# Longer fillings on TensorE at sixteen places, and sparse attention with its minima and exponentials one pair ahead and its value products two behind

## The chip, the cores and the metric

The kernel runs on one core of a Trainium2 chip. The time is the device time of one execution in microseconds (us). TensorE does the matrix products, VectorE (DVE in the rows), ScalarE (ACT) and GpSimd (POOL) the rest, SyncE starts the transfers. The trace gives, for every stretch, the clock that TensorE was granted, as a share of 2.4 GHz: it is either 1.00 (2.4 GHz) or 0.50 (1.2 GHz), and a mean between the two says how the stretch divides.

## The reference

The program is a small network on 512 tokens of width 1024, batch 1: two layers of a first block (attention, a gated delta net, convolution, a feed-forward net, with an RMS norm ahead of and behind each half), one layer with a recurrent time mix and a feed-forward net, and one with sparse attention, a short convolution and a mixture of experts. Cut to the parts that the change touches:

```
def rms_norm(x, w):   y = x * rsqrt(mean(x*x) + eps);  return y * w

# first block, for l in range(2)
h = rms_norm(x, pre_mix);   u = h @ w_in;  ...  y = mixers(u) @ w_out
x = x + rms_norm(y, post_mix)
h = rms_norm(x, pre_mlp);   y = square(relu(h @ w_ff1)) @ w_ff2
x = x + rms_norm(y, post_mlp)

# sparse attention of the last layer: 8 query heads, 2 key heads of 64, 512 tokens
for each head:
    o_cmp = softmax(masked(q @ k_cmp.T)) @ v_cmp      # 31 compressed keys
    o_slc = softmax(masked(q @ k_slc.T)) @ v_slc      # causal, up to 512 keys
    o_win = softmax(masked(q @ k_win.T)) @ v_win      # causal, up to 512 keys
    y = g0 * o_cmp + g1 * o_slc + g2 * o_win
```

## The kernel before

All is float32; the large products are made of three products of rounded halves (`high`, `low`; L501 to L503), tile by tile of 128 x 512. The network is a row of **phases**. A phase (L165) is a block in which each engine has its own list of instructions, tied by semaphores; at its end all engines meet twice (L169, L172), and no engine starts the next phase before the slowest has arrived.

**Fillings.** `fill_in` (L235) issues n products of a constant 128 x 128 tile into a bank that nobody reads. They compute nothing. They stand where TensorE has no work and waits for others. They are in TensorE's list, so the phase can't end before they are done. The change alters these counts:

- `rms_norm` (L242): TensorE adds up the squares (L286), then fills (L289) while ScalarE takes the root (L278) and VectorE makes the reciprocal (L300) and eight products (L306). With `add_to` (behind each feed-forward net of the first block: twice) VectorE makes eight more sums (L311), and the filling is twice as long. Without `add_to` it is called seven times: ahead of the two first-block layers, ahead of both halves of the last two layers, and at the very end.
- `add_norm` (L315, twice): the norm behind the mixers, the addition, and the next norm in one phase; its second filling is L362.
- `linear` (L409) with a `source`: at its start ScalarE and VectorE split the first weights (L518, L561) and the source (L554, L597), and TensorE fills (L507). If the first weights were already split in the phase before (`primed == SPLIT`) only the source is left to do. The two calls with `LOADED` are the output projections of the last two layers (L2230, L2798).
- `compress` (L2289): the filling L2399, while VectorE makes the short convolution (L2281, L2285).

**Sparse attention** (L2420) goes over 4 **tiles** j of two heads each, in each over 4 query blocks t, and for each over 2 branches: 32 **pairs** q, each a pair of heads. Eight pairs make a tile; t grows from 0 to 3 within it, two pairs each, and the work of a pair is (t + 1) x 128 keys wide. For each pair:

- `scored` (TensorE, L2583 and L2586): the scores, into two of four score banks. It runs two pairs ahead and waits until `exponent` of the pair that had the banks is done.
- `top` (VectorE, L2711): the minimum of each row. `exponent` (ScalarE, L2490): the exponentials.
- `transposed` (TensorE, L2597): turns them, into two banks. `take_turned` copies the first bank on ScalarE (L2499), the second on VectorE (L2720), into `turned`.
- `apply` (TensorE, L2615; for every other pair L2610 too, the compressed branch): the products with the values, into a product bank of a **group** (the two branches of one query block). There are two product banks; the next group but one waits for `rows_done` of the older.
- per group: `weigh` (VectorE, L2727 to L2732), `first_part` (ScalarE, L2517), `other_parts` (VectorE, L2740, L2745; gives `rows_done`), `turn_rows` (TensorE, L2624), `take_rows` (ScalarE, L2523).
- per tile, for the next one: `rotate` and `scale_query` at the tile's first pair, `score_c` and `top_of_c` at its third, `exponent_c` and `mask_c` at its fourth, `turn_c` and `take_turned_c` at its fifth and seventh (L2510).

The order on each engine is written out by hand in a loop over q. TensorE in step q (L2637): `scored(q + 2)`, the tile's or group's extra work, `apply(q - 1)`, a filling of one product (L2666), `transposed(q)`.

## Time and profile before

| | us |
|---|---|
| runs (three) | 4427.88, 4421.81, 4433.57; median 4427.88 |
| the profiled execution, its own time | 4435.43 |
| its span, first to last instruction | 4433.5 |
| TensorE busy | 4132.3 (93%) |
| VectorE, ScalarE busy | 1579.9, 1300.1 |
| mean granted clock over the span | 0.933 |
| sparse attention, first to last matrix product | 3293.57 to 3487.27 |

The span is nearly the whole time; what lies around it is 1.9 us. "Busy" on TensorE includes the fillings. A matrix product takes twice as long at clock 0.50, so a stretch can be busy and slow at once: the busy share must be read together with the granted clock. In the rows, `x30` is the number of instructions merged into one row, the bracket at the end is the idle time of the engine ahead of it and what ended it, and `PEq L172` is the meeting of all engines at a phase's end. A matrix product in plain float32 is counted as two instructions, one in rounded halves (L239, L501) as one.

### The profile page before, as it was taken

How to read it: one execution, taken by the hardware profiler on the slowest of the kernel's cores; microseconds unless marked ns; L12 is line 12 of the kernel's file. 1: busy time of each engine (PE TensorE's matmuls, PEld its weight loads, DVE VectorE, ACT ScalarE, POOL GpSimd, SP SyncE). 2: the span in 40 equal slices, each digit the busy share in tenths (PEclk: the TensorE clock that was granted, in tenths of full speed). 3: DMA queues.
4: the chain of work that ended last, by engine and by line, in shares of the span. 5: the costliest groups of instructions: out<-in, count | busy, mean ns of one | idle time of the engine just before them, and what ended most of it. 6: DMA issues, size and time to landing. Idle time of an engine off the chain costs nothing. (4 is left out here: it accounts for less than half of the span.)

```text
span 4433.5 us, 57036 instructions
## 1 busy us (share of the span) xinstructions
PE 4132.3 (93%) x22339; PEld 3461.1 (78%) x22339; DVE 1579.9 (36%) x2702; ACT 1300.1 (29%) x2253; POOL 206.9 (5%) x169
## 2 busy tenths in 40 slices
PE   8999999999999999999997899999988889999999
PEld 5787876777678887677765777787756689999998
DVE  2365535233236553523326543332233421111212
ACT  2364533231246453323123322221213311111111
POOL 0151100000024100000000000000000000000000
PEclk9998989999999898999998899999987889999999
DMA  3100012221200001222120012232220034454443
GB/s 121 43 1 1 0 38 76 93 86 49 93 33 1 1 0 38 86 85 95 57 85 15 1 39 76 81 105 68 96 76 1 21 127 161 176 193 164 156 168 125
DMA packets 51478, 324.88 MB, mean 73 GB/s; under 512 B 6528, under 2 KB 7424, under 8 KB 20352
## 3 DMA queue, kind: packets, MB, share of 16 engines
q1 hardware_dynamic: 51328, 322.85, 20.7%
q8 instruction: 98, 1.61, 0.1%
q14 instruction: 52, 0.43, 0.0%
HBM read 319.68 MB, written 2.10 MB: 73 GB/s over the span
## 5 line engine op out<-in xcount | busy, mean ns | idle before, releaser
L501 PE MATMUL bank<-high 128*128 128x512 f32 x2480 | 976.5, 394 | 43.9 <-DVEq L591 22.8
L502 PE MATMUL bank<-low,high 128*128 128x512 f32 x2480 | 973.8, 393 | 0.0
L503 PE MATMUL bank<-high,low 128*128 128x512 f32 x2480 | 972.6, 392 | 0.0
L501 PEld LDWEIGHTS bank<-high 128*128 128x128 f32 x2480 | 471.4, 190 | 149.8 <-DVEq L591 25.6
L503 PEld LDWEIGHTS bank<-high,low 128*128 128x128 f32 x2480 | 470.9, 190 | 99.4
L502 PEld LDWEIGHTS bank<-low,high 128*128 128x128 f32 x2480 | 471.3, 190 | 97.8
L561 DVE TENSOR_TENSOR low<-weight_ring,high 128x2048 fp32r<-128x2048 f32 (+1 forms) x144 | 319.3, 2218 | 545.8 <-ACT high L518 545.8
L3110 PE MATMUL bank<-chosen,glu_ring 128*128 128x176 f32 x2816 | 422.0, 313 | 0.0
L3110 PEld LDWEIGHTS bank<-chosen,glu_ring 128*128 128x128 f32 x2816 | 420.1, 190 | 0.0
L518 ACT ACTIVATE high<-weight_ring 128x2048 fp32r<-128x2048 f32 (+1 forms) x144 | 266.7, 1854 | 266.8 <-PE bank L503 233.0
L239 PE MATMUL bank<-filler 128*128 128x512 f32 x819 | 247.6, 446 | 23.9 <-PEq L172 23.2
L239 PEld LDWEIGHTS bank<-filler 128*128 128x128 f32 x819 | 167.7, 209 | 77.5 <-issue 41.3
L3121 PE MATMUL bank<-hidden,down_ring 128*128 128x176 f32 x1408 | 211.3, 313 | 0.0
L3121 PEld LDWEIGHTS bank<-hidden,down_ring 128*128 128x128 f32 x1408 | 210.4, 190 | 0.0
L1414 DVE TENSOR_TENSOR joint<-bank,level_masks 128x512 f32<-128x512 f32 x224 | 153.9, 691 | 146.7 <-PE bank L1433 146.7
L741 POOL TENSOR_TENSOR y<-y,scaled 128x512 f32<-128x512 f32 x120 | 149.8, 1277 | 1007.7 <-ACT scaled L775 1007.7
L3199 DVE TENSOR_TENSOR hidden<-silu,bank 128x176 f32<-128x176 f32 x88 | 29.8, 338 | 390.6 <-ACT silu L3167 390.6
L569 DVE TENSOR_TENSOR gated<-gated,bank 128x512 f32<-128x512 f32 x86 | 59.0, 686 | 285.0 <-ACT gated L525 159.0
L3167 ACT ACTIVATE silu<-bank 128x176 f32<-128x176 f32 x88 | 27.9, 318 | 445.8 <-PE bank L3110 445.8
L1446 PE MATMUL bank<-weight_ring,joint 128*128 128x128 f32 x1152 | 151.8, 276 | 0.0
L622 ACT ACTIVATE u<-bank 128x512 f32 (+1 forms) x84 | 50.3, 599 | 330.4 <-PE bank L503 330.4
L1446 PEld LDWEIGHTS bank<-weight_ring,joint 128*128 128x128 f32 x1152 | 139.5, 192 | 0.9
(497 smaller groups left out, 4904.6 us busy)
## 6 DMA issues: line engine op xcount, KB each, us to landing
glu_ring<-in_w_expert SPq DMA_DIRECT2D x88, 1024.0 KB, 4.9
weight_ring<-in_w_ff SPq DMA_DIRECT2D x64, 1024.0 KB, 5.0
down_ring<-in_w_expert_down SPq DMA_DIRECT2D x64, 704.0 KB, 5.0
weight_ring<-in_w_in SPq DMA_DIRECT2D x22, 1024.0 KB, 4.8
weight_ring<-in_w_ffe SPq DMA_DIRECT2D x22, 1024.0 KB, 4.9
weight_ring<-in_w_downe SPq DMA_DIRECT2D x16, 704.0 KB, 4.1
weight_ring<-in_w_ino SPq DMA_DIRECT2D x11, 1024.0 KB, 4.8
weight_ring<-in_w_ine SPq DMA_DIRECT2D x9, 1024.0 KB, 5.0
```

Of the source, the lines that this page charges most:

```text
L239: nc.tensor.matmul(bank[:, :], tile, tile.unsqueeze(1).broadcast_to([P, SEQ // P, P]), start=True, stop=True)
L501: nc.tensor.matmul(mem.bank[b][:, :], whole, high[:, k, :], start=(k == 0), stop=False)
L502: nc.tensor.matmul(mem.bank[b][:, :], whole, low[:, k, :], start=False, stop=False)
L503: last = nc.tensor.matmul(mem.bank[b][:, :], rest, high[:, k, :], start=False, stop=(k == kt - 1))
L518: nc.scalar.activation(w_high[:, s, :], mem.ring[:, s, 0:size], ACT.Copy).then_inc(high_ready[s], 1)
L561: nc.vector.tensor_tensor(w_low[:, s, :], mem.ring[:, s, 0:size], w_high[:, s, :], ALU.subtract).then_inc(low_ready[s], 1)
L569: nc.vector.tensor_tensor(whole, whole, mem.bank[b][:, :], ALU.mult).then_inc(taken[b], 1)
L741: nc.gpsimd.tensor_tensor(y[:, c, :], y[:, c, :], scaled[:, n % CONV_SLOTS, :], ALU.add).then_inc(added, 1)
L1414: nc.vector.tensor_tensor(chunks(joint[:, n, :]), chunks(turn_bank(i)[:, :]), mask, ALU.mult) \
L1446: last = nc.tensor.matmul(product_bank(i)[:, c], joint[:, n, c], matrix[:, n, c], start=True, stop=True)
L3110: last = nc.tensor.matmul(two(low[s])[:, half, :], glu_ring[:, s, at:at + P], chosen[:, k, :], start=(k == 0), stop=(k == KD - 1))
L3121: last = nc.tensor.matmul(two(high[m // 2])[:, m % 2, :], down_ring[:, s, k * P:(k + 1) * P], hidden[:, k, :], start=(k == 0), stop=(k == ...
```

## The change

Three things. Fillings: 30 products become 42 and 60 become 84 in the norms, 5 become 12 in `linear` where the first weights are loaded only, 30 become 52 in `compress`, and sparse attention gets two new fillings at its start (4 behind `rotate(0)`, 8 behind `score_c(0)`). Second, the order of VectorE and ScalarE in sparse attention: `top` and `exponent` are called one pair further ahead, and `take_turned` of a pair in its own step. Third, TensorE applies pair q - 2 instead of q - 1 in step q, with `turned` six wide instead of four, and waits for `high_taken` ahead of the filling, a wait that `apply(q - 1)` held before.

```diff
@@ rms_norm
-            fill_in(nc, mem, mem.bank[1], 30 if add_to is None else 60)
+            fill_in(nc, mem, mem.bank[1], 42 if add_to is None else 84)
@@ add_norm
-            fill_in(nc, mem, mem.bank[2], 30)
+            fill_in(nc, mem, mem.bank[2], 42)
@@ linear
-                fill_in(nc, mem, mem.bank[n_banks - 1], 5)
+                fill_in(nc, mem, mem.bank[n_banks - 1], 5 if primed == SPLIT else 12)
@@ compress
-            fill_in(nc, mem, turn_banks[0], 30)
+            fill_in(nc, mem, turn_banks[0], 52)
@@ sparse_attention, ScalarE
-                if q >= 2:
-                    act.wait_ge(applied, q - 1)
-                nc.scalar.activation(turned[:, 2 * q % 4, 0:width], ...
+                if q >= 3:
+                    act.wait_ge(applied, q - 2)
+                nc.scalar.activation(turned[:, 2 * q % 6, 0:width], ...
...
+            exponent(0)
             for q in range(n_pairs):
                 j, at = divmod(q, per_tile)
-                exponent(q)
+                if q + 1 < n_pairs:
+                    exponent(q + 1)
...
-                if q >= 1:
-                    take_turned(q - 1)
...
                 if q >= 7 and q % 2:
                     take_rows((q - 7) // 2)
-                if q >= 4 and q % 2 == 0:
-                    first_part((q - 4) // 2)
+                take_turned(q)
+                if j + 1 < tiles and at == 3:
+                    exponent_c(j + 1)
+                if q >= 5 and q % 2:
+                    first_part((q - 5) // 2)
@@ sparse_attention, TensorE
             rotate(0)
+            fill_in(nc, mem, turn_banks[0], 4)
             pe.wait_ge(rot_taken, 1)
             score_c(0)
+            fill_in(nc, mem, mem.bank[6], 8)
...
-                if q >= 1:
-                    apply(q - 1)
+                if q >= 2:
+                    apply(q - 2)
...
+                if q >= 1:
+                    pe.wait_ge(high_taken, q)
                 fill_in(nc, mem, turn_banks[0], 1)
                 transposed(q)
+            apply(n_pairs - 2)
             apply(n_pairs - 1)
@@ sparse_attention, VectorE
+            top(0)
             for q in range(n_pairs):
                 j, at = divmod(q, per_tile)
-                top(q)
+                if q + 1 < n_pairs:
+                    top(q + 1)
+                if j + 1 < tiles and at == 2:
+                    top_of_c(j + 1)
+                take_turned(q)
+                if j + 1 < tiles and at == 3:
+                    mask_c(j + 1)
                 if q >= 4 and q % 2 == 0:
                     weigh((q - 4) // 2)
...
-                if q >= 4 and q % 2 == 0:
-                    other_parts((q - 4) // 2)
+                if q >= 5 and q % 2:
+                    other_parts((q - 5) // 2)
```

Two places show what that does to the lists. First VectorE in the second half of a tile, before; `tops` are the minima, `turned` the copies, `weights` belong to `weigh`, `part` and `rows` to `other_parts`:

```order
L2711 TENSOR_REDUCE tops<-bank 128x1 x2
L2720 COPY turned<-bank 128x384
L2711 TENSOR_REDUCE tops<-bank 128x1 x2
L2727 TENSOR_SCALAR weights<-bank 128x6
L2729 RECIPROCAL weights<-weights 128x6
L2732 TENSOR_TENSOR weights<-weights,gate 128x6
L2720 COPY turned<-bank 128x384
L2740 SCALAR_TENSOR_TENSOR part<-bank,weights,part 128x64 x2
L2745 SCALAR_TENSOR_TENSOR rows<-bank,weights,part 128x64 x2
L2711 TENSOR_REDUCE tops<-bank 128x1 x2
```

The same place with the change (its line numbers are up to five higher there: L2716 is L2711, L2725 is L2720, L2732 to L2737 are `weigh`, L2745 and L2750 `other_parts`):

```order
L2716 TENSOR_REDUCE tops<-bank 128x1 x2
L2725 COPY turned<-bank 128x384
L2745 SCALAR_TENSOR_TENSOR part<-bank,weights,part 128x64 x2
L2750 SCALAR_TENSOR_TENSOR rows<-bank,weights,part 128x64 x2
L2716 TENSOR_REDUCE tops<-bank 128x1 x2
L2725 COPY turned<-bank 128x512
L2732 TENSOR_SCALAR weights<-bank 128x6
L2734 RECIPROCAL weights<-weights 128x6
L2737 TENSOR_TENSOR weights<-weights,gate 128x6
L2716 TENSOR_REDUCE tops<-bank 128x1 x2
```

Minima and copies still alternate, as they did. What moved is `weigh`, now behind a copy, and `other_parts`, now behind the other copy, one pair later. Next ScalarE at the tile's fifth to seventh pair, before; `probs` are the exponentials, `turned_c` is `take_turned_c`, `part` is `first_part`, `y` is `take_rows`:

```order
L2490 ACTIVATE probs<-bank,tops 128x384 x2
L2499 ACTIVATE turned<-bank 128x256
L2510 ACTIVATE turned_c<-bank 31x512
L2517 ACTIVATE part<-bank,weights 128x64 x2
L2490 ACTIVATE probs<-bank,tops 128x384 x2
L2499 ACTIVATE turned<-bank 128x384
L2523 ACTIVATE y<-bank 128x128
```

The same with the change:

```order
L2490 ACTIVATE probs<-bank,tops 128x384 x2
L2510 ACTIVATE turned_c<-bank 31x512
L2499 ACTIVATE turned<-bank 128x384
L2490 ACTIVATE probs<-bank,tops 128x512 x2
L2523 ACTIVATE y<-bank 128x128
L2499 ACTIVATE turned<-bank 128x384
L2517 ACTIVATE part<-bank,weights 128x64 x2
```

Exponentials and copies alternate as before; `take_turned_c` and `take_rows` have moved from behind a copy to behind the next pair's exponentials.

## Rows read from the trace of the kernel before

**Rows 1.** The page: busy time by engine, and the granted clock in 40 slices.
```profile
PE 4132.3 (93%) x22339; PEld 3461.1 (78%) x22339; DVE 1579.9 (36%) x2702; ACT 1300.1 (29%) x2253; POOL 206.9 (5%) x169
PEclk9998989999999898999998899999987889999999
```
**Rows 2.** Timeline of the first norm (start, duration, engine, line): PE and DVE.
```profile
24.56 7.41 PE L239 MATMUL bank<-filler 128*128 128x512 f32 x30
25.88 3.35 DVE L300 RECIPROCAL scale<-scale 128x512 f32<-128x512 f32 x1 [8.47 <-ACT scale L278]
29.33 5.39 DVE L306 SCALAR_TENSOR_TENSOR h_branch<-x_res,vec,scale 128x512 f32<-128x512 f32 x8
35.73 6.55 PE L647 MATMUL bank<-w_tm,h_branch 128*128 128x408 f32 x11 [3.76 <-PEq L172]
```
**Rows 3.** Busy time in stretches: length, then each engine, granted clock, DMA share, GB/s.
```profile
35.73:40.80 5.07, 5.07 (x8) 2.67 (x9) 0.00 (x0) 0.10 (x1) 0.00 (x0) 0.50 0.75 281
2205.70:2211.60 5.90, 5.90 (x7) 2.45 (x8) 1.68 (x3) 1.31 (x3) 0.00 (x0) 0.50 0.95 349
527.94:530.28 2.34, 0.00 (x0) 0.03 (x1) 1.38 (x3) 0.00 (x0) 0.99 (x1) 1.00 0.00 0
530.30:540.00 9.70, 9.70 (x86) 9.55 (x87) 5.12 (x8) 6.75 (x15) 2.56 (x2) 1.00 0.00 0
...
3113.00:3116.20 3.20, 3.20 (x8) 2.30 (x8) 0.00 (x0) 0.00 (x0) 0.00 (x0) 0.50 0.99 404
```
**Rows 4.** Timeline around the two norms with `add_to`: PE and DVE.
```profile
1092.75 14.21 PE L239 MATMUL bank<-filler 128*128 128x512 f32 x60
1102.96 4.91 DVE L311 TENSOR_TENSOR x_res<-x_res,squares 128x512 f32<-128x512 f32 x8
1113.19 8.55 PE L286 MATMUL bank<-squares,const_cols 128*128 128x512 f32 x16 [6.22 <-DVE squares L296]
...
2205.63 10.16 PE L286 MATMUL bank<-squares,const_cols 128*128 128x512 f32 x16 [3.06 <-DVE squares L296]
```
**Rows 5.** Timeline of PE at both output projections and at the start of sparse attention.
```profile
2641.94 0.76 PE L501 MATMUL bank<-high 128*128 128x512 f32 x1 [3.58 <-DVE low L597]
...
3488.47 2.47 PE L239 MATMUL bank<-filler 128*128 128x512 f32 x5 [1.21 <-PEq L172]
...
3293.57 2.05 PE L2555 MATMUL bank<-u,const_cols 128*128 128x512 f32 x2 [6.52 <-PEq L172]
```
**Rows 6.** Who PE waited for in sparse attention: us in total, times, longest.
```profile
PE bank L2583 <- ACT probs L2490: 14.7, 11, 2.1
```
**Rows 7.** Busy time in stretches of the loop over pairs, columns as in rows 3.
```profile
3300.66:3487.28 186.62, 166.23 (x870) 125.32 (x870) 68.07 (x224) 61.21 (x160) 11.43 (x9) 0.74 0.00 1
3433.70:3440.50 6.80, 6.80 (x32) 5.93 (x31) 0.56 (x1) 1.47 (x3) 0.00 (x0) 0.50 0.01 2
3382.50:3403.00 20.50, 20.50 (x90) 17.41 (x89) 4.91 (x14) 5.78 (x14) 0.75 (x1) 0.50 0.01 1
3450.80:3478.00 27.20, 25.00 (x171) 18.95 (x170) 14.90 (x47) 11.97 (x34) 0.00 (x0) 1.00 0.00 1
```
**Rows 8.** Timeline at the fifth to seventh pair of the third tile.
```profile
3429.28 0.38 PE L2597 MATMUL bank<-const_cols,probs 128*128 128x128 f32 x2
...
3429.89 1.01 DVE L2711 TENSOR_REDUCE tops<-bank 128x1 f32<-128x384 f32 x2
3430.47 1.05 ACT L2490 ACTIVATE probs<-bank,tops 128x384 f32<-128x384 f32 x2 [1.62 <-DVE tops L2711]
3430.82 0.55 DVE L2720 COPY turned<-bank 128x384 f32<-128x384 f32 x1
...
3431.58 1.13 PE L2583 MATMUL bank<-u,q_rot 64*128 64x512 f32 x4 [1.92 <-ACT probs L2490]
...
3440.36 1.54 PE L2615 MATMUL bank<-values,turned 128*128 128x65 f32 x12
3440.60 0.59 ACT L2510 ACTIVATE turned_c<-bank 31x512 f32<-31x512 f32 x1 [2.35 <-PE bank L2569]
3441.09 0.48 ACT L2517 ACTIVATE part<-bank,weights 128x64 f32<-128x64 f32 x2
...
3441.71 0.48 DVE L2740 SCALAR_TENSOR_TENSOR part<-bank,weights,part 128x64 f32<-128x64 f32 x2 [2.75 <-ACT part L2517]
```

More of the change, by code:

```diff
@@ L2433, in sparse_attention @@
     with buffers(nc, q_rot=[P, 2, SEQ], turn=[P, SEQ], values=[P, TT, 2 * C_KV, wide], vc=[P, C_KV, wide],
-                 gate=[P, TT, C_HEADS * N_BRANCH], probs=[P, 4, SEQ], turned=[P, 4, SEQ], probs_c=[P, 2, TT, N_CMP],
+                 gate=[P, TT, C_HEADS * N_BRANCH], probs=[P, 4, SEQ], turned=[P, 6, SEQ], probs_c=[P, 2, TT, N_CMP],
                  top_c_rows=[P, 2 * TT], turned_c=[P, 2, 2, SEQ], tops=[P, 2 * n_pairs], weights=[P, n_groups, 2, N_BRANCH],
@@ L2496, in take_turned @@
                 act.wait_ge(turn_out, 2 * q + 1)
-                if q >= 2:
-                    act.wait_ge(applied, q - 1)
-                nc.scalar.activation(turned[:, 2 * q % 4, 0:width], turn_banks[0][:, 0:width], ACT.Copy) \
+                if q >= 3:
+                    act.wait_ge(applied, q - 2)
+                nc.scalar.activation(turned[:, 2 * q % 6, 0:width], turn_banks[0][:, 0:width], ACT.Copy) \
                     .then_inc(high_taken, 1)
@@ L2537, in _ @@
                         scale_query(j + 1)
-                    elif at == 3:
-                        exponent_c(j + 1)
                     elif at in (4, 6):
@@ L2543, in _ @@
                     take_rows((q - 7) // 2)
-                if q >= 4 and q % 2 == 0:
-                    first_part((q - 4) // 2)
-            take_turned(n_pairs - 1)
+                take_turned(q)
[3 more added lines that the diff above has]
+                    first_part((q - 5) // 2)
             for g in range(n_groups - 2, n_groups):
@@ L2614, in apply @@
                     for b in range(t + 1):
-                        last = nc.tensor.matmul(product(g, h, 1 + branch), turned[:, (2 * q + h) % 4, b * P:(b + 1) * P],
+                        last = nc.tensor.matmul(product(g, h, 1 + branch), turned[:, (2 * q + h) % 6, b * P:(b + 1) * P],
                                                 values[:, b, branch * C_KV + kv_of(j), :], start=(b == 0), stop=(b == t))
@@ L2716, in take_turned @@
                 dve.wait_ge(turn_out, 2 * q + 2)
-                if q >= 2:
-                    dve.wait_ge(applied, q - 1)
+                if q >= 3:
+                    dve.wait_ge(applied, q - 2)
                 width = (t + 1) * P
-                nc.vector.tensor_copy(turned[:, (2 * q + 1) % 4, 0:width], turn_banks[1][:, 0:width]).then_inc(low_taken, 1)
+                nc.vector.tensor_copy(turned[:, (2 * q + 1) % 6, 0:width], turn_banks[1][:, 0:width]).then_inc(low_taken, 1)
             def weigh(g):
@@ L2761, in _ @@
             dve.wait_ge(gate_ready, 1)
+            top(0)
             for q in range(n_pairs):
                 j, at = divmod(q, per_tile)
-                top(q)
+                if q + 1 < n_pairs:
[5 more added lines that the diff above has]
+                    mask_c(j + 1)
                 if q >= 4 and q % 2 == 0:
                     weigh((q - 4) // 2)
-                if q >= 1:
-                    take_turned(q - 1)
-                if j + 1 < tiles:
-                    if at == 2:
-                        top_of_c(j + 1)
-                    elif at == 3:
-                        mask_c(j + 1)
-                if q >= 4 and q % 2 == 0:
-                    other_parts((q - 4) // 2)
-            take_turned(n_pairs - 1)
+                if q >= 5 and q % 2:
+                    other_parts((q - 5) // 2)
             for g in range(n_groups - 2, n_groups):
```

## Prediction

> **What bounds the kernel now.** I read the page first: TensorE is busy 93% of the span, and the granted clock is below 9 tenths in many of the 40 slices [rows 1]. So the time is TensorE's, and there are two ways to lose some: TensorE idles, or it works at 1.2 GHz. The mean clock of 0.933 (the table) says that 13% of the span is at the lower level. Then I looked where that is, with the timeline of TensorE and VectorE around every filling, and the stretches' granted clock behind it.
>
> At the first norm the filling of 30 ends at 31.97, VectorE's last product at 34.72, and TensorE resumes at 35.73 [rows 2], 1.01 after VectorE. TensorE has been idle for 3.76, and its next 5.07 us run at clock 0.50 [rows 3]. Work that would take half as long: 2.5 us lost. An idle stretch of 2.34 elsewhere left the clock at 1.00, in it and behind it [rows 3]. So shortening 3.76 to about 1 should keep the clock.
>
> In sparse attention the loop over pairs takes 186.6 us at a mean clock of 0.74, which is 97 us at 0.50; TensorE is shown busy for 166.2 of it [rows 7]. It waits 14.7 us in total for ScalarE's exponentials, eleven times [rows 6]. One such wait, seen in the timeline [rows 8]: the turning of pair 5 ends at 3429.66, the next scores start 1.92 later, because VectorE's minima (3429.89) stood behind `other_parts`, which stood behind `first_part`, which stood behind `take_turned_c`, which waited for TensorE itself. Four microseconds on the clock is 0.50 for 6.8 us [rows 7].
>
> **Part 1, fillings of 42.** One filling costs what 30 more add in the norm with 60: (14.21 - 7.41) / 30 = 0.227 us [rows 2, 4]. Twelve more take 2.72. The first norm's filling then ends at 34.69, 0.03 ahead of VectorE. All these phases have the same chain on VectorE (3.35 and 5.39 [rows 2]), so they come out alike, within 0.3 us, and the idle stretch falls to about 1.05. What hides the fillings is VectorE's chain; if it were shorter, each 0.1 us would be on the path. What comes back is half of the time that the next phase works at clock 0.50. It is 5.07 at the first norm and 5.7 at the time-mix layer's norm: 2.5 + 2.9. It is 3.4 at the second layer's norm, behind each `add_norm`, 3.2 at the sparse layer's norm [rows 3] and 2.7 at the feed-forward norm: 1.7 + 2 x 1.7 + 1.6 + 1.3. Sum 13.4 saved. At the norm ahead of the mixture the idle stretch is 6.7 and stays about 4, and behind the last norm there is no TensorE work: nothing.
>
> **Part 2, fillings of 84.** In the norm with `add_to` the filling of 60 ends at 1106.96, VectorE at 1107.87 [rows 4]. That idle stretch was 0.9 us long, and 24 more take 5.44, to 1112.4. VectorE has nothing left to hide the last 4.5, and the phase can't end before TensorE's list does. I take 4.3 us for the meeting's own slack, twice: + 8.6. What may come back: behind the first one TensorE is idle 6.22 [rows 4], much of it the jump back to the loop's start, of which about 5 stay, so the clock falls as before. Behind the second it is idle 3.06 and then 5.90 at clock 0.50 [rows 3, 4]; with the longer filling about 1.9 idle remain, which by the stretch of 2.34 keeps the clock [rows 3]: - 2.9. Net + 5.7.
>
> **Part 3, fillings of 12 and 52, and the start of sparse attention.** At the time-mix layer's output projection TensorE idles 3.58 [rows 5] and then works 3.2 at 0.50; seven more fillings leave 2.0: - 1.6. At the sparse layer's the five fillings already run at 0.50 (2.47 for 5 [rows 5]), so seven more take 3.0 against an idle stretch of 2.5, which costs up to 0.5, and the clock may rise sooner for up to - 2.6; I take - 0.4. In `compress` 22 more take 5.0 of the 6.52 idle [rows 5]; the rotation of 2.05 at half clock becomes about 1.05, and the compressed scores behind it (1.9) about 1.0, of which 1.7 stand on the path: - 1.7. The new 4 and 8 lie in waits of that start (0.9 and 1.8 us for them at full clock; the wait before the first scores is 2.3).
>
> The Trainium skill ("TensorE: Matmul & The Clock Gate", section "Why this matters for your kernels") advises to have no idle gap of TensorE above about 3 us between bursts of products. The falls behind 3.76 agree with it. It would make the idle stretches of 1.9 us in sparse attention harmless, and there the trace disagrees: the clock falls behind a 1.92 idle stretch in a loop of narrow products, so the measurement decides.
>
> **Part 4, the loop over pairs.** The rows of the order show that minima, exponentials and copies alternate as before; "one ahead" renames the steps. What really moves: (a) `take_turned_c` and `first_part` no longer stand between a pair's copy and the next pair's minima in even steps: the chain behind the 14.7 us goes. (b) `take_rows` and `take_turned_c` now stand behind the next exponentials, and TensorE waits for both ahead of its filling. (c) `apply(q - 2)` opens a group's product bank one copy after `other_parts`, which is now late. I put the new waits together from the durations there [rows 8], counted from the end of a turning. At a tile's fifth pair: ScalarE and VectorE copy (0.4), `exponent_c` and `first_part` (0.4 + 0.48), `other_parts` (2 x 0.48), minima and exponentials (about 0.6 and 1.05), `take_turned_c` (0.59), with handovers 4.7; TensorE has scores (1.13 + 0.3), the turning of the compressed branch 0.4, the products with 0.6 and 0.85, together 3.3. So 1.4 idle. The seventh pair gives 4.7 against 3.0: 1.7. The odd pairs wait for `take_rows`: copy 0.4 to 0.6, `weigh` 0.66, minima and exponentials 1.0 to 2.0, 0.28, against 1.8 to 2.8: 0.3 to 1.2 each, 2.6 in a tile. That is 6 us in each of tiles 2 and 3, about 3 in the first, about 5 in the last (where before there was about 1), and 2 more at the end, where `apply(30)` waits for `other_parts`: 22 us idle in all against some 19 now. Nothing is gained in idle time; it costs about 3.
>
> What may be gained is clock. The idle stretches are shorter (1.1 to 1.7 against 1.6 to 2.1) and, at half clock, vanish: TensorE's own work between the links doubles to over 6 us, more than the chain's 4.7. Today the chain through TensorE keeps waits even at half clock, and two slow episodes last 20.5 and 17 us [rows 7]. I expect episodes of some 7 us instead: of 97 us at 0.50 about 26 go, worth 13. Net - 10. Bounds: at best no slow episode, 97 / 2 x 166 / 187 = 43 less, with 3 more idle: - 40. At worst + 21 (the third rival).
>
> **Sum.** -13.4 + 5.7 - 1.6 - 0.4 - 1.7 - 10 = -21.4. Against the profiled execution's own 4435.4 that is 4414.0. The median of the runs shown is 7.5 below that execution, so the forecast for the median is 4406.5.
>
> **Rivals.** (1) *The even spacing holds the clock up nearly everywhere in the loop.* For it: in the last tile, with waits of 0.3, 27.2 us ran at 1.00 [rows 7]. Against: that was with hardly any wait. Loop - 40: 4376. (2) *The order gives nothing*: the new waits fall where the old ones were and the clock falls as often. For it: the same idle sum, and 1.4 to 1.7 is near to 1.6. Loop 0: 4416; where stretches this short don't move the clock at all and only the idle sum counts, + 3: 4419. (3) *Slower*: TensorE waits for `rows_done` in the last tile, where no work of a next tile covers it: copy 0.5, `first_part` 0.48, `other_parts` 0.96, with handovers 2.1 from the turning's end, against scores of 0.9 to 1.4. That is 0.6 to 1.3 at each even pair and 2.1 at the last. If one of these suffices to bring the clock down, the 27.2 us now at 1.00 take 12.5 more, idle adds 8, and the other tiles give nothing: loop + 21, total + 9.6, 4437. It decides from an idle stretch of about 1.6 in that tile. (4) *The fillings of 42 end behind VectorE* by 1 us, because they start later or run at half clock: 4413.
>
> The Trainium skill's rule above, taken as it stands, leads to the second form of rival 2, since every idle stretch of the loop is below 3 us; the row behind the 1.92 stretch speaks against it, which is why that form has only 0.05 of rival 2's chance.
>
> **How the numbers follow.** Forecast 0.50, own range 4396 to 4417; rival 1 0.10; rival 2 0.23; rival 3 0.11; rival 4 0.06. A measurement of this kernel tells about 0.3%, or 13 us, from no change: faster means below 4414.6. The forecast gives 0.44 of its 0.50 to faster, rival 1 all, rival 2 a third, rival 4 half: 0.65. Slower (above 4441) is a part of rival 3 and two fillings of 84 that cost more: 0.05. Same 0.30. The range 4386 to 4431 leaves out most of rival 1 and of rival 3.
>
> **What would show it.** Right: in the changed profile the work behind the seven fillings of 42 at clock 1.00, idle about 1.05 ahead of it; at both norms with `add_to` TensorE the last to arrive, 4 to 4.5 us after VectorE; in the loop no wait for exponentials ahead of the scores but waits of 0.3 to 1.7 ahead of the filling and ahead of L2610, and a mean clock of 0.8 to 0.85. Wrong: a loop at 0.74 or below, or above 0.95; a phase with `add_to` as long as before; VectorE's chain ending before the filling of 42.

## The result

Five executions of the changed kernel, beside five of the kernel before on the same chip:

| | before | changed |
|---|---|---|
| median of five | 4427.29 us | 4401.81 us |
| range | 4421.81 to 4433.57 | 4382.84 to 4404.85 |
| ratio, 95% interval | | 0.9928 [0.9902, 0.9954] |
| profiled execution | 4435.43 | 4386.44 |
| mean granted clock | 0.933 | 0.949 |
| at clock 0.50, whole span | 595.7 us | 445.8 us |

The change saves 25.5 us by the medians (forecast 21.4). The profiled execution is 15.4 below its kernel's median, and that of before 8.1 above its own, so the two traces together show 49 us, about twice what the change is worth. Phase lengths that do not depend on the clock can be compared directly; sums over the whole span can't. Of the runs below, one execution of e2 (7781 us) and one of e3 (6948 us) lie far from all others and are left out of every median and ratio.

The page of the changed kernel, busy time and clock, against [rows 1]:

```profile
PE 4121.8 (94%) x22543; PEld 3457.9 (79%) x22543; DVE 1579.6 (36%) x2702; ACT 1300.8 (30%) x2253; POOL 206.4 (5%) x169
PEclk9998989999999899999998889999999889999999
```

TensorE does more instructions (the longer fillings) in less busy time. That is possible because it does more of them at clock 1.00.

**Behind the norms.** The timeline at the first norm, against [rows 2], and stretches from this kernel's answer (columns: stretch, length, busy time of PE, PEld, DVE, ACT, POOL with counts, clock, DMA share, GB/s), against [rows 3]:

```profile
25.82 7.87 PE L239 MATMUL bank<-filler 128*128 128x512 f32 x34
34.77 1.61 PE L647 MATMUL bank<-w_tm,h_branch 128*128 128x408 f32 x4 [1.08 <-PEq L172]
```
```profile
33.69:40.00 6.31, 5.23 (x17) 2.98 (x17) 0.07 (x1) 0.39 (x1) 0.00 (x0) 1.00 0.65 241
```

The idle stretch ahead of L647 fell from 3.76 to 1.08 us, and the work behind it is at clock 1.00 instead of 0.50. At the three other norms whose next phase begins with L647 it is 1.03, 1.02 and 1.06, without a fall.

**The norms with `add_to`.** The second of them, against [rows 4]:

```profile
2170.07 19.65 PE L239 MATMUL bank<-filler 128*128 128x512 f32 x84
2180.28 4.91 DVE L311 TENSOR_TENSOR x_res<-x_res,squares 128x512 f32<-128x512 f32 x8
2191.62 1.55 PE L286 MATMUL bank<-squares,const_cols 128*128 128x512 f32 x3 [1.90 <-DVE squares L296]
```
```profile
2170.07:2193.00 22.93, 21.03 (x89) 16.43 (x88) 15.77 (x21) 2.88 (x5) 0.00 (x0) 1.00 0.07 13
```

VectorE ends at 2185.19 and TensorE's filling at 2189.72, 4.53 us later: everybody waits for products that compute nothing. The phase takes 29.44 us where it took 25.15 (+4.29), the other one 29.42 (+4.28). The idle stretch behind is 1.90 instead of 3.06 and the clock stays, so the next phase is 3.01 shorter. Behind the first one the idle stretch is still 5.53, and the clock falls.

**The output projection** of the time-mix layer, where seven more products left an idle stretch of 2.01:

```profile
2621.62 2.97 PE L239 MATMUL bank<-filler 128*128 128x512 f32 x12 [0.90 <-PEq L172]
2626.60 0.68 PE L501 MATMUL bank<-high 128*128 128x512 f32 x1 [2.01 <-DVE low L597]
```
```profile
2626.70:2630.10 3.40, 3.40 (x9) 2.63 (x10) 3.40 (x7) 2.79 (x3) 0.00 (x0) 0.50 0.86 301
```

Here the clock fell all the same and the phase kept its length, 51.85 against 51.83. In e4 and e5 below it fell too, behind 1.97 and 1.99 idle; in the nine other kernels with twelve fillings here, behind 1.96 to 1.99, it stayed and the phase was 1.6 shorter. So behind an idle stretch of 2 us the clock may fall or not.

**Sparse attention.** From the first to the last matrix product it takes 164.5 us instead of 193.7:

```profile
3277.40:3441.87 164.47, 148.26 (x900) 111.22 (x900) 73.30 (x237) 65.26 (x164) 11.33 (x9) 0.87 0.00 1
3422.40:3428.40 6.00, 6.00 (x26) 5.45 (x27) 1.12 (x2) 1.88 (x3) 0.00 (x0) 0.50 0.00 0
```

and what TensorE waits for in it (us in total, times, longest), against [rows 6]:

```profile
PE bank L2610 <- DVE rows L2750: 6.5, 9, 1.8
PE bank L239 <- ACT y L2523: 4.5, 5, 1.0
PE bank L239 <- ACT turned_c L2510: 1.4, 5, 0.3
```

No wait for exponentials is left. In its place stand three: for the rows of the group before the last (ahead of L2610), and for two small copies of ScalarE ahead of the filling. The timeline of the last tile shows one of each, against [rows 8]:

```profile
3417.94 1.28 ACT L2490 ACTIVATE probs<-bank,tops 128x512 f32<-128x512 f32 x2 [1.53 <-DVE tops L2716]
3419.12 0.27 ACT L2523 ACTIVATE y<-bank 128x128 f32<-128x128 f32 x1
3419.44 0.50 PE L239 MATMUL bank<-filler 128*128 128x512 f32 x1 [0.83 <-ACT y L2523]
3419.78 0.82 PE L2597 MATMUL bank<-const_cols,probs 128*128 128x128 f32 x6
3420.31 0.49 ACT L2499 ACTIVATE turned<-bank 128x384 f32<-128x384 f32 x1 [0.92 <-PE bank L2597]
3420.70 0.51 ACT L2517 ACTIVATE part<-bank,weights 128x64 f32<-128x64 f32 x2
3421.34 0.47 DVE L2745 SCALAR_TENSOR_TENSOR part<-bank,weights,part 128x64 f32<-128x64 f32 x2
3421.85 0.48 DVE L2750 SCALAR_TENSOR_TENSOR rows<-bank,weights,part 128x64 f32<-128x64 f32 x2
3422.38 1.11 PE L2610 MATMUL bank<-vc,turned_c 31*128 31x65 f32 x4 [1.78 <-DVE rows L2750]
```

Read it downwards. `take_rows` (L2523) stands behind two exponentials, and TensorE's filling waits 0.83 for it. Then the turning ends at 3420.60, copy, `first_part` and `other_parts` follow one another, and the value products start at 3422.38, 1.78 later, at clock 0.50 (the second stretch above).

The gain is not spread evenly. Cut at the last tile's first scores, the first three tiles take 97.0 us where they took 137.6, with 10 us at clock 0.50 for 86; the last one takes 62.1 where it took 49.0, with 33.5 us at clock 0.50 for 11.4. Changed, then before:

```profile
3282.78:3379.77 96.99, 88.96 (x585) 64.72 (x585) 44.77 (x142) 42.63 (x108) 11.33 (x9) 0.95 0.00 1
3379.77:3441.87 62.10, 54.23 (x287) 43.08 (x286) 24.11 (x82) 19.40 (x53) 0.00 (x0) 0.73 0.00 1
```
```profile
3300.66:3438.29 137.63, 123.78 (x600) 91.36 (x600) 45.59 (x149) 43.02 (x110) 11.43 (x9) 0.69 0.00 1
3438.29:3487.27 48.98, 42.45 (x271) 33.97 (x270) 22.48 (x75) 18.19 (x50) 0.00 (x0) 0.88 0.00 1
```

### The profile page after: what moved, and what is told of

Same layout as the page of the kernel before. It is cut to its first block and busy times, and to the rows that moved or that the text cites. A ratio compares the mean times of both kernels' runs of the same rounds, so it can differ in the third digit from the quotient of the medians.

```text
span 4384.2 us, 57466 instructions
## 1 busy us (share of the span) xinstructions
PE 4121.8 (94%) x22543; PEld 3457.9 (79%) x22543; DVE 1579.6 (36%) x2702; ACT 1300.8 (30%) x2253; POOL 206.4 (5%) x169
## 5 line engine op out<-in xcount | busy, mean ns | idle before, releaser
L239 PE MATMUL bank<-filler 128*128 128x512 f32 x1023 | 291.9, 432 | 21.8 <-PEq L172 15.1
L239 PEld LDWEIGHTS bank<-filler 128*128 128x128 f32 x1023 | 205.2, 204 | 85.1 <-issue 34.4
```

The lines of the kernel that those rows point to most:

```text
L239: nc.tensor.matmul(bank[:, :], tile, tile.unsqueeze(1).broadcast_to([P, SEQ // P, P]), start=True, stop=True)
```

## The experiments

Each was timed in five rounds beside the kernel before, whose median was 4431.83, 4424.79 and 4431.68 us in the three groups of runs (e1 to e4, e5 to e8, e9 to e12). Kernels of different groups are compared by their ratios to it, not by their medians. "Stage" is the phase of sparse attention in the profiled execution, "low" its time at clock 0.50, "idle" the sum of TensorE's idle stretches above 0.1 us from the first turning of a pair to the last product. "Three tiles" and "last tile" divide the stage from its first scores to its last product at the last tile's first scores (which TensorE makes two pairs ahead); in brackets is the last tile's time at clock 0.50. Each of these columns is from one profiled execution.

| | median us | ratio [95%] | stage | low | idle | three tiles | last tile (low) |
|---|---|---|---|---|---|---|---|
| before | | | 194.9 | 106.1 | 18.9 | 137.6 | 49.0 (11.4) |
| changed | 4401.81 | 0.9928 [0.9902, 0.9954] | 165.6 | 44.3 | 14.1 | 97.0 | 62.1 (33.5) |
| e1 fillings only | 4410.45 | 0.9955 [0.9936, 0.9974] | 208.3 | 135.7 | 17.1 | 139.7 | 62.1 (41.6) |
| e2 order only | 4409.81 | 0.9950 [0.9933, 0.9966] | 171.3 | 65.5 | 13.3 | 101.0 | 62.1 (33.6) |
| e3 changed, 64 for 84 | 4374.03 | 0.9871 [0.9841, 0.9901] | 167.3 | 47.0 | 14.4 | 95.5 | 65.4 (39.6) |
| e4 e1, value products two behind | 4380.27 | 0.9893 [0.9868, 0.9917] | 152.4 | 20.6 | 12.4 | 100.8 | 45.0 (3.4) |
| e5 changed, again | 4395.15 | 0.9923 [0.9899, 0.9947] | 176.2 | 68.3 | 14.1 | 107.5 | 62.2 (33.7) |
| e6 e4, 64 for 84 | 4363.43 | 0.9856 [0.9837, 0.9875] | 152.9 | 21.5 | 13.2 | 102.8 | 43.6 (0.5) |
| e7 e3, 36 for 42 | 4375.96 | 0.9888 [0.9869, 0.9908] | 165.5 | 45.5 | 13.0 | 96.3 | 62.7 (34.7) |
| e8 e3, fillings in the last tile | 4369.55 | 0.9877 [0.9858, 0.9896] | 157.4 | 20.3 | 12.0 | 96.3 | 54.6 (9.6) |
| e9 e3, parts earlier | 4405.57 | 0.9945 [0.9925, 0.9966] | 195.1 | 99.0 | 19.7 | 117.6 | 70.9 (58.6) |
| e10 e3, small copies first | 4369.79 | 0.9862 [0.9833, 0.9891] | 149.7 | 25.6 | 8.7 | 87.6 | 55.6 (21.7) |
| e11 e9 and e10 | 4365.17 | 0.9855 [0.9825, 0.9885] | 154.3 | 20.5 | 13.7 | 100.0 | 47.7 (6.8) |
| e12 e6, again | 4362.95 | 0.9832 [0.9808, 0.9856] | 149.4 | 15.7 | 12.5 | 99.3 | 43.6 (1.5) |

### The two halves apart

e1 is the kernel before with every filling of the change and its own order. e2 is the new order with the old fillings:

```diff
 e2, against the changed kernel
-            fill_in(nc, mem, mem.bank[1], 42 if add_to is None else 84)
+            fill_in(nc, mem, mem.bank[1], 30 if add_to is None else 60)
 (also 42 -> 30 in add_norm, 12 -> 5 in linear, 52 -> 30 in compress, no 4 and 8)
```

> The order in sparse attention as before; all fillings as in the change (42, 84, 12, 52 and the new 4 and 8). Theory A (the loop's gain is the order's): the phases outside sparse attention as in the changed profile, with both add_to phases 4.3 us longer and the work behind each filling of 42 at clock 1.00; in the loop over pairs about 20 us of idle TensorE and waits of 1.6 to 2.1 us for exponentials as before, 80 to 98 us at clock 0.50; the stage of sparse attention from barrier to barrier about 187 to 191 us (194.85 before, 165.63 changed). Total about 4415 to 4420. Theory B (the loop's gain comes from the warm start that the fillings give): the stage 165 to 175 us, total about 4400.

> The changed order in sparse attention, every filling as before (30, 60, 5, 30, none at the start). Theory A: the stage 168 to 173 us (3 to 5 lost again at its cold start), the loop with about 16 us idle and 45 to 60 us at clock 0.50; the two add_to phases as before, the seven idle stretches ahead of products 3.76 us again and 1.2 GHz behind them. Total about 4400 to 4408. Theory B: the stage 185 to 195 us, total about 4425.

Each half gives about 0.5%, and the two ratios together (1 - 0.0045 - 0.0050 = 0.9905) lie just within the interval of the whole. That each half helps without the other is shown; that they add up exactly is not. Nothing shows the fillings alone helping the loop: in e1's profile sparse attention is even slower than before, at the same order,

```profile
3270.92:3478.04 207.12, 188.35 (x900) 140.54 (x900) 72.46 (x237) 64.52 (x164) 11.41 (x9) 0.67 0.00 1
```

That execution was the slowest of e1's eleven, so this one profile does not say what the loop takes on average; it says that the same order can take 194.9 or 208.3 us.

### The norms with `add_to`

```diff
 e3, against the changed kernel
-            fill_in(nc, mem, mem.bank[1], 42 if add_to is None else 84)
+            fill_in(nc, mem, mem.bank[1], 42 if add_to is None else 64)
```

> The changed kernel with 64 fillings instead of 84 in the norms with add_to. If the 84 overran VectorE's chain, as the two barriers 4.28 us later say, each of these two phases gets back to within 0.2 us of its length before: 8.5 us less, of which up to 3 are given back where the idle stretch behind the second becomes 2.3 instead of 1.9 us and the clock falls again. Total 5 to 8.5 below the changed kernel, about 4394 to 4397. The rival says that the longer filling pays by its clock: total the same or higher.

The two phases take 25.14 and 23.44 us with 64 products, 29.42 and 29.44 with 84: 10.3 us less. 1.7 of it is a fall of the clock during the sums, which the second escaped; at the same clock (27.74 in e4, 23.44 in e6, each twice) twenty products make 4.3, twice 8.6. The profiles differ by 8.4 (changed and e3) and 6.0 (e4 and e6), the ratios by 25 and 16 us. With some 0.3% (13 us) either side of each ratio both reach down to 8.6; whether more than that is in it stays open.

### Which part of the order gives the gain

e4 takes from the change only what TensorE does; VectorE and ScalarE keep the order of before:

```diff
 e4, against e1
-                 turned=[P, 4, SEQ]   (and % 4 -> % 6 at its three uses)
+                 turned=[P, 6, SEQ]
-                if q >= 2:
-                    act.wait_ge(applied, q - 1)      (dve alike)
+                if q >= 3:
+                    act.wait_ge(applied, q - 2)
-                if q >= 1:
-                    apply(q - 1)
+                if q >= 2:
+                    apply(q - 2)
...
+                if q >= 1:
+                    pe.wait_ge(high_taken, q)
                 fill_in(nc, mem, turn_banks[0], 1)
                 transposed(q)
+            apply(n_pairs - 2)
             apply(n_pairs - 1)
```

> Fillings as in the change; in sparse attention only TensorE's value products two pairs behind (turned six wide), VectorE and ScalarE in their order of before. Theory A1 (the gain is that other_parts, first_part and the compressed copy no longer stand between a copy and the next minima): the waits for exponentials of 1.6 to 2.1 us stay, the stage 187 to 193 us as with the fillings alone. Theory A2 (the products two behind are what counts): the stage 165 to 175 us.

> The changed kernel as it is, as a control on the same chip as the next three. If phases differ from run to run only by where the clock falls, the stage of sparse attention lies within 10 us of 165.6, both add_to phases at 29.4 us, and the total at 4385 to 4405.

> Fillings of the change with 64 for 84, TensorE's value products two behind, VectorE and ScalarE in their order of before. Theory (the fine cost of 84 is 4.3 us twice, and the reordering of minima and exponentials costs rather than gains): the stage 150 to 158 us as in the run with the 84, the add_to phases 25.1 us or, at full clock, 23.5; total 6 to 9 below that run, about 4372, and about 15 below the changed kernel with 64. Rival (the 152.4 us of that one profile were luck of the clock): the stage 160 to 170 us, total 4385.

With TensorE's part alone the stage takes 152.4 us, less than either theory said, against 165.6 and 176.2 for two executions of the whole change. e6, the same with 64, and its repeat e12 are by their medians the fastest kernels of the study, and the steadiest: nine executions from 4356.24 to 4364.32. Its stretch and its waits:

```profile
3268.23:3419.96 151.73, 136.67 (x900) 101.39 (x900) 73.79 (x237) 64.74 (x164) 11.44 (x9) 0.93 0.00 1
```
```profile
PE bank L2583 <- ACT probs L2490: 10.3, 9, 1.7
PE bank L2624 <- ACT y L2523: 1.4, 1, 1.4
PE bank L239 <- ACT turn L2481: 0.7, 1, 0.7
```

The waits for exponentials of [rows 6] are still there, but 10.3 us instead of 14.7, and the longest 1.7 instead of 2.1. Nothing waits ahead of L2610 any more, nor ahead of a filling but once for 0.7. So value products two behind are enough for the gain (e1 to e4, intervals apart). That the new order of VectorE and ScalarE takes part of it back is what the stages show (13 us or more) and the ratios allow: e4 against the changed kernel and e6 against e3 have overlapping intervals. The last column says where. In every profile with that order as it is (changed, e2, e3, e5, e7) the last tile takes 62.1 to 65.4 us; with TensorE's part alone (e4, e6, e12) 43.6 to 45.0. In the first three tiles the new order is no slower: 95.5 to 101.0, and 107.5 once, against 99.3 to 102.8.

### Fillings shorter, and fillings in the last tile

```diff
 e7, against e3
-            fill_in(nc, mem, mem.bank[1], 42 if add_to is None else 64)
+            fill_in(nc, mem, mem.bank[1], 36 if add_to is None else 64)
-            fill_in(nc, mem, mem.bank[2], 42)
+            fill_in(nc, mem, mem.bank[2], 36)
 e8, against e3, in TensorE's loop ahead of apply(q - 2)
+                if j + 1 == tiles and at % 2 == 0:
+                    pe.wait_ge(high_taken, q)
+                    fill_in(nc, mem, turn_banks[0], 6 if at == 6 else 4)
```

> The changed kernel with 36 fillings for 42 in the norms and 64 for 84. TensorE's idle stretches ahead of the products become 2.4 us, near to the stretch of 2.34 that kept its clock in the profile of before. If that holds, the work behind stays at 1.00 and the total equals the changed kernel with 64 (about 4376 to 4394). If the clock falls behind 2.4 us, up to 13 us are lost again, wholly or at those of the seven places where it falls.

> The changed kernel with 64 for 84 and, in the last tile's even pairs, 4 more fillings (6 at the last) ahead of the value products, where TensorE idles 0.8 to 1.8 us for rows_done. If these idle stretches bring the clock down in the last tile (24 us at 0.50 in the changed profile), that tile stays at 1.00 and the stage is 8 to 12 us shorter, 155 to 160. If not, the stage is as before or 1 us longer.

With 36 products the idle stretches ahead of L647 are 2.40. Behind the first norm the clock fell,

```profile
35.25 7.07 PE L647 MATMUL bank<-w_tm,h_branch 128*128 128x408 f32 x15 [2.40 <-PEq L172]
```
```profile
36.50:39.90 3.40, 3.40 (x7) 1.71 (x6) 0.00 (x0) 0.00 (x0) 0.00 (x0) 0.50 0.86 347
```

and behind the three others that end so it did not. The time can't be told from e3's: six products fewer cost 1.7 us once, which no interval here can show. In e8 the fillings stand in the very stretches in which TensorE waited for `rows_done`; only the first (0.51) and the one behind the loop (1.78) stay. The last tile takes 54.6 us with 9.6 at clock 0.50, where the five profiles without the fillings agree on 62.1 to 65.4 with 33.5 to 39.6, although the fillings shorten no chain: they stand where TensorE idled. The ratios don't settle what it is worth (0.9877, against 0.9871 for e3 and 0.9888 for e7).

### What the new order of VectorE and ScalarE costs

```diff
 e9, against e3 (ScalarE; other_parts on VectorE alike, directly behind weigh)
-                if q >= 5 and q % 2:
-                    first_part((q - 5) // 2)
+                if q >= 4 and q % 2 == 0:
+                    first_part((q - 4) // 2)
 e10, against e3 (ScalarE)
+                if j + 1 < tiles and at in (4, 6):
+                    take_turned_c(j + 1, (at - 4) // 2)
+                if q >= 7 and q % 2:
+                    take_rows((q - 7) // 2)
                 if q + 1 < n_pairs:
                     exponent(q + 1)
...
-                    elif at in (4, 6):
-                        take_turned_c(j + 1, (at - 4) // 2)
-                if q >= 7 and q % 2:
-                    take_rows((q - 7) // 2)
                 take_turned(q)
 e11: both
```

> The changed kernel with 64 in both norms with add_to (the kernel of e3_add_to_64), and first_part and other_parts of a group moved one pair earlier, to the even steps directly behind take_turned and weigh (where the kernel before had them relative to weigh). Question: which part of the new order of VectorE and ScalarE costs the 13 us or more that the kernel with only TensorE's two-behind order has over it in sparse attention (152 to 153 us against 165 to 176). Theory P (other_parts is too late: TensorE waits 6.5 us in nine places for its rows ahead of L2610, 1.78 twice in the last tile): those nine waits go entirely, the clock keeps up in the last tile, the stage comes down from 167 to 155 to 160 us, ratio about 0.985 to 0.986, near 4364. Theory C (it is the small copies behind the exponentials, for which the filling waits): the waits ahead of L2610 go but the stage stays above 163 and the time within 4370 to 4380. Theory N: other_parts now delays the next minima as in the kernel before, a wait of about 1 for exponentials comes back at each even pair, idle time stays at 16 and the stage at 165 or above.

> The kernel of e3_add_to_64 with take_turned_c (of the next tile) and take_rows moved ahead of exponent(q + 1) on ScalarE. Theory C (TensorE waits 4.8 us in six places for y and 1.4 in five for turned_c ahead of its filling because both copies stand behind two exponentials): these waits go, the exponentials start up to 0.5 later, which nothing waits for, idle falls from 16 to about 10 and the stage from 167 to 155 to 160 us, about 4366. Theory P: the waits of 1.8 ahead of L2610 stay and bring the clock down, stage 163 or above, 4370 to 4380. Theory N: the exponentials are now late instead and the idle sum is unchanged.

> Both edits of e9_parts_earlier and e10_small_copies_first on the kernel of e3_add_to_64. If the two late pieces are the whole cost of the new order of VectorE and ScalarE: idle TensorE in the loop below 10 us, under 25 us at clock 0.50, stage 150 to 154 us, and the time 4358 to 4364, as with TensorE's part alone (4363.4) or below it. If minima and exponentials one pair ahead cost something by themselves (Theory N): stage 158 or more, 4368 or more.

> The kernel of e6_two_behind_64 once more, beside the three others on the same chip. All theories: 4358 to 4366, ratio 0.985 to 0.987, stage 152 to 156 us with 20 to 30 us at clock 0.50. If its stage comes out at 162 or above, the comparison of one profile each was luck and the order of VectorE and ScalarE may cost nothing.

e9 is the miss that teaches most. The nine waits for rows went, as theory P said, but the kernel lost 0.7% against e3 (0.9945 and 0.9871, intervals apart); of the three theories only N, that the parts delay the minima, allows a stage of 195.1 us. Its waits, and the timeline of one:

```profile
PE bank L239 <- ACT y L2523: 16.3, 10, 2.7
```
```profile
3364.91 0.48 DVE L2750 SCALAR_TENSOR_TENSOR rows<-bank,weights,part 128x64 f32<-128x64 f32 x2
3365.31 1.01 DVE L2716 TENSOR_REDUCE tops<-bank 128x1 f32<-128x384 f32 x2
3365.89 1.05 ACT L2490 ACTIVATE probs<-bank,tops 128x384 f32<-128x384 f32 x2 [1.62 <-DVE tops L2716]
3366.83 0.28 ACT L2523 ACTIVATE y<-bank 128x128 f32<-128x128 f32 x1
3367.16 0.50 PE L239 MATMUL bank<-filler 128*128 128x512 f32 x1 [2.66 <-ACT y L2523]
```

`other_parts` now delays the minima, the minima the exponentials, and behind the exponentials stands a copy of 0.28 us for which TensorE waits 2.66. The exponentials themselves are early enough, one pair ahead; only the small copy behind them is late. e10 takes just that copy (and `take_turned_c`) out from behind them: the waits ahead of the filling are gone, those ahead of L2610 are still there,

```profile
PE bank L2609 <- DVE rows L2749: 7.0, 10, 1.8
```
```profile
3266.66:3415.21 148.55, 137.79 (x900) 105.27 (x900) 73.40 (x237) 65.49 (x164) 11.35 (x9) 0.92 0.01 1
```

(its lines are one lower), and the stage takes 149.7 us, as short as with TensorE's part alone. So theory C holds for the first three tiles: without the small copies' waits they take 87.6 us for 95.5, the shortest of all. In the last tile the late rows cost too. There e10 still waits 1.79 and 1.68 for them, the clock is at 0.50 for 27.3 us from 1.1 behind the first of the two, and the tile takes 55.6 against 43.6 to 45.0 for e4, e6 and e12. e11, with the rows earlier as well, brings the last tile to 47.7, but twelve waits for exponentials (11.3 us) are back and the first three tiles take 100.0. The late parts are thus right in the first three tiles and wrong in the last; late parts there and early ones here, or e10 with e8's fillings, was not run. By the medians all this is less clear than in the profiles: e10's six executions fall into three of 4359 to 4361 and three of 4378 to 4386, e11's likewise into four of 4355 to 4366 and two of 4385 to 4386. What the upper ones lose was not profiled. e12 shows no such upper ones, and none of e10, e11 and e12 can be told from the others by their intervals. The version to take is e6: it and its repeat beat the changed kernel (0.9856 and 0.9832 against 0.9928 and 0.9923, intervals apart); it saves 1.4 to 1.7% in all.

## Why the prediction was right, and where it wasn't

**Part 1, fillings of 42: right in each row.** 0.227 us for one product, idle about 1.05 behind (measured 1.02 to 1.08), clock kept. Phase by phase, in us, forecast and measured: first norm's next phase 2.5 and 2.55; second layer 1.7 and 1.69; behind each `add_norm` 1.7 and 2.0; time-mix layer 2.9 and 2.91; feed-forward norm 1.3 and 1.3; sparse layer 1.6 and 1.68. Sum 13.4 and 14.1. Rival 4 is out: the fillings of the first norm end at 33.69 and VectorE's last product at 33.76, as close together as forecast, both a microsecond earlier, since the phase began 0.5 earlier and its sums ran wholly at clock 1.00 (1.5 us of them at 0.50 before). Two norm phases themselves moved, in opposite directions: the one ahead of the mixture went from 20.2 to 18.5 here and in e4 to e8 and e11, but stayed at 20.2 in e1, e3, e9, e10 and e12 with the same filling; the sparse layer's went from 18.5 to 20.2, its sums now at half clock, and did so in all kernels but e2, e8 and e11. So such 1.7 come and go from run to run, and here they cancel.

**Part 2, fillings of 84: right.** + 8.6 forecast, + 8.57 measured; - 2.9 forecast behind the second, - 3.01 measured. Behind the first the clock fell as said, and the phase even grew by 1.4. The forecast came out of one subtraction in the profile: the fillings had 0.9 us of cover left and got 5.44 more. e3 and e6 confirm it from the other side.

**Part 3: signs right, sizes exchanged.** The time-mix layer's projection was to give 1.6 and gave 0 (a fall behind 2.01 idle; in nine later kernels it gave 1.6). The sparse layer's was to give 0.4 and gave 2.42: twelve fillings end 0.65 ahead of the work. The step that failed there is the choice between the bounds: up to 0.5 lost and up to 2.6 saved, and I took the middle. At the start of sparse attention the first scores stand 5.38 behind the first product instead of 7.09: 1.7, as forecast. The phase of `compress` itself gave 0.7 more.

**Part 4, the loop: direction right, size and half of the reason wrong.** Forecast - 10; the two profiles of the change give - 29 and - 19 for the stage, and e2's ratio makes the order alone worth 22 us (15 to 30). Three steps:

- *"take_turned_c and first_part no longer stand between a pair's copy and the next pair's minima: the chain behind the 14.7 us goes."* It goes, but that is not the main gain: e4 leaves this chain in and takes 100.8 us for the first three tiles, the changed kernel 97.0, because the waits for small copies stand in the chain's place (e10, without them: 87.6). What helps is that the value products of two pairs back, with L2610 and their filling, are ready work while the chain runs. I had listed that as (c), and only as a cost.
- *"take_rows and take_turned_c now stand behind the next exponentials, and TensorE waits for both"* (b): right, and by e10 some 8 us in the first three tiles and 10 in the last.
- *1.4 and 1.7 us idle at the fifth and seventh pair*: measured 0.5 and 0.8 in tiles 2 and 3. I had added each instruction's duration with a handover; in the trace neighbours overlap, a copy of the turned scores starts 0.3 us before the turning ends (above, ScalarE at 3420.31), and the next instruction before the last has ended. The forecast idle sum of 22 us became 14.1 (before: 18.9). With stretches of 1.6 to 2.1 replaced by many below 1, time at clock 0.50 in the loop fell from 98 to 44 us, where 71 was forecast. That the shorter stretches are the reason is the likely reading, not one that a run isolates.

Rival 3's mechanism is real: TensorE waits for `rows_done` in the last tile, 1.78 us twice, and the clock fell near both (at 3422.0 for 6.8 us and at 3435.6 for 10.2). The longest episode of that tile (17.1 us from 3394.7) began behind a wait of only 0.78 (L2610 at 3392.1). The last tile lost 13.1 us against the profile before; its time at clock 0.50 grew by 22.1, worth 11.1 us, near the 12.5 that rival 3 gave for the clock. What failed in the rival is its 8 us of added idle time there and "the other tiles give nothing": they gave 40.6. (e1 has the order of before and took 62.1 for its last tile as well, so the loss is sure only against e4, e6 and e12.) e8 shows that filling those stretches takes about half of that loss away. The row on which rivals 1 and 3 lean was misread: the 27.2 us at clock 1.00 in the last tile held idle stretches of 0.61 and 1.26, not only 0.3. So the loop's gain in the profiles is a large one in the early tiles and a loss in the last, where - 10 was forecast for the whole by episodes of some 7 us instead of 20. Rival 1 (loop - 40, little low time at all) is not the changed kernel but e4, e6, e10 and e12: 15 to 26 us low in the stage, which is 42 to 46 shorter.

The median came out at 4401.81 for 4406.5. Fillings alone were forecast at - 11.4 and measured by e1 at - 20 (- 11 to - 28), the order at - 10 and by e2 at - 22 (- 15 to - 30); both were short, and the whole, at - 25.5, is less than their sum though within its interval. So the close hit of the total is partly luck.

The Trainium skill ("TensorE: Matmul & The Clock Gate", section "Why this matters for your kernels") advises to have no idle gap above about 3 us. The rows above put it lower for this kernel: falls behind 2.01, behind 2.40 in one case of four, and in the last tile behind 1.78 and even 0.78. Single stretches of 1.02 to 1.08 behind the norms never led to one. So the length of one stretch alone does not decide here.

## What to carry to other kernels

Before a filling is lengthened, read in the timeline which engine arrives last and by how much: up to there each filling product was free here, and with it the clock held behind all seven norms; from there each cost more than 0.2 us, for nothing. In a loop of short links give TensorE work that is older than the link it waits for, and keep any small copy for which TensorE waits ahead of the long operation of its engine, not behind it. Look at the last round of a loop by itself: there no work of a next round covers a late link, and an order that is best in the others can be the worst there. Change one engine's order at a time; here TensorE's part earned 27 us by the ratios (e1 to e4), and the other engines' part cost 13 to 14 us of the stage (e6 to e3, e4 to the changed kernel), which is 7 and 16 us by the ratios and not clear of their intervals.

## What the runs showed of the chip

- The loss by the clock is not one number for one kernel. The phase of sparse attention with the same instructions in the same order took 165.6 and 176.2 us in two profiled executions, with 44 and 68 us at clock 0.50; with TensorE's part alone it took 152.4, 152.9 and 149.4. The spread of the runs was 22 and 32 us for the change (five and six executions) and 8 for e6 and e12 together. Less idle time alone does not make it steady: e10 has the least and a spread of 27.
- A slow episode can last long. In e9's stage one lasted 51.2 us (from 3378.2), in e1's 34.1 (from 3424.8), with idle stretches of 1.2 to 2.7 ahead of it and in it; in e6's none was above 6.8.
- The same instructions of one phase took 25.9, 27.5 and 29.1 us in three kernels (e2, changed, e4), with none, 3.4 and 6.8 us at clock 0.50. Such steps, and larger ones (25.1 and 31.1 for a phase of the time-mix layer before and in the changed kernel), stand all over the comparison of two traces, in phases that the change does not touch, and cancel only roughly; they say nothing about the change.
